# FFN entry of a one-core decoder layer: the first chunk's up tiles as a quad of seven block products

## The reference, cut to what matters

```python
hn = rms_norm(x, g_pre_ffn[l])
gu = jnp.einsum('bsd,df->bsf', hn, w_gate_up[l])
hf = jax.nn.silu(gu[..., :D_FF]) * gu[..., D_FF:]
ff = jnp.einsum('bsf,fd->bsd', hf, w_down[l])
x = x + rms_norm(ff, g_post_ffn[l])
```

## Time and profile before

| | us |
|---|---|
| median of 3 runs (1764.28 to 1937.19) | 1764.4 |
| the profiled execution | 1763.94 |
| its span | 1762.4 |
| TensorE busy | 1752.1 (99%) |
| VectorE busy | 1132.3 (64%) |
| ScalarE busy | 733.2 (42%) |
| GpSimd busy | 249.7 (14%) |

### The profile page before, as it was taken

The page is one execution under the profiler, slowest core; times in us unless marked ns, Lnnn a source line. Parts: engine busy times, 40 slices in busy tenths (PEclk is TensorE's granted clock), DMA queues, the critical chain, the costliest instruction groups (busy, mean ns, idle before and its releaser), DMA issues.

```text
span 1762.4 us, 23988 instructions
## 1 busy us (share of the span) xinstructions
PE 1752.1 (99%) x8497; PEld 1453.7 (82%) x8497; DVE 1132.3 (64%) x1927; ACT 733.2 (42%) x1486; POOL 249.7 (14%) x555
## 2 busy tenths in 40 slices
PE   9999999999999999999999999999999999999998
PEld 7888888888888888888888888888888888888886
DVE  5328888888775774443555655776656655567676
ACT  5316666666643233343221123343333333344553
POOL 3321222222210001111100112101011000000011
PEclk9999999999999999999999999999999999999999
DMA  7421222222143223337635712223233322673443
GB/s 244 144 85 57 76 74 73 73 73 72 49 144 95 72 66 130 104 102 259 219 132 167 240 60 83 96 96 142 93 111 109 105 89 102 228 279 100 145 143 126
DMA packets 138047, 213.80 MB, mean 121 GB/s; under 512 B 7569, under 2 KB 94097, under 8 KB 136930
## 3 DMA queue, kind: packets, MB, share of 16 engines
q1 hardware_dynamic: 109200, 108.54, 19.6%
q0 software_dynamic: 28752, 104.04, 16.2%
q10 hardware_dynamic: 2, 0.00, 0.0%
HBM read 150.17 MB, written 62.39 MB: 121 GB/s over the span
## 4 chain that ended last, share of the span: by engine, by line
PE 98%; DVE 1%; ACT 1%; DMA 0%; issue 0%; POOL 0%; POOLq 0%; DVEq 0%; ACTq 0%
PE ps L2343 26%; PE ps L2678 22%; PE ps L2546 17%; PE ps L2734 12%; PE ps L2427 10%; PE ps L2351 3%; PE ps L2443 3%; PE ps L2465 2%; PE ps L2467 1%; DVE ring L1564 0%; DMA x_tile<-in_x_dram 0%; ACT e_t L1089 0%; ACT ring L968 0%; DVE e_t L1667 0%; DVE d_op L1564 0%
## 5 line engine op out<-in xcount | busy, mean ns | idle before, releaser
L2734 PE MATMUL ps<-d_op 128*128 128x512 f32 x924 | 210.3, 389 | 0.1
L2734 PEld LDWEIGHTS ps<-d_op 128*128 128x128 f32 x924 | 173.3, 188 | 36.8 <-DVE d_op L1564 0.5
L2678 PE MATMUL ps<-s_op,t_op_T 128*128 128x512 f32 x720 | 169.9, 389 | 0.0
L2427 PE MATMUL ps<-xn,ring 128*128 128x512 f32 x672 | 167.0, 398 | 0.0
L2678 PEld LDWEIGHTS ps<-s_op,t_op_T 128*128 128x128 f32 x720 | 135.1, 188 | 28.1
L2427 PEld LDWEIGHTS ps<-xn,ring 128*128 128x128 f32 x672 | 122.3, 188 | 24.2
L2546 PE MATMUL ps<-s_op,x_op_T 128*128 128x512 f32 x576 | 135.9, 389 | 0.0
L2546 PEld LDWEIGHTS ps<-s_op,x_op_T 128*128 128x128 f32 x576 | 108.1, 188 | 22.5
L2678 PE MATMUL ps<-hn,t_op_B 128*128 128x512 f32 x480 | 115.1, 389 | 0.0
L2678 PEld LDWEIGHTS ps<-hn,t_op_B 128*128 128x128 f32 x480 | 90.1, 188 | 18.7
L1676 DVE CUSTOM_DVE_ANT_0 ps<-ps,mask 128x256 f32<-128x256 f32 (+7 forms) x128 | 94.5, 780 | 12.2 <-PE ps L2443 11.1
(11 more groups left out here) (270 smaller groups left out, 3361.4 us busy)
## 6 DMA issues: line engine op xcount, KB each, us to landing
pair<-in_w_gate_up_dram SPq DMA_DIRECT2D x20, 1024.0 KB, 5.2
rf_pieces<-s_scratch SPq DMA_DIRECT2D x74, 256.0 KB, 2.6
x_pair<-in_w_in_dram SPq DMA_DIRECT2D x16, 1024.0 KB, 6.7
raw<-in_w_in_dram SPq DMA_DIRECT2D x26, 512.0 KB, 4.0
s_scratch<-gated_ff POOLq DMA_DIRECT2D x40, 256.0 KB, 2.5
gate_in<-gate_scratch POOLq DMA_DIRECT2D x18, 512.0 KB, 3.6
v_scratch<-v_out POOLq DMA_DIRECT2D x32, 256.0 KB, 2.6
vh<-v_scratch POOLq DMA_DIRECT2D x16, 512.0 KB, 5.1
```

The costliest lines, as they stand in the source:

```text
L2427: last = pe.matmul(ps[:, proj_bank(first, half), :], proj_weights(which, par, a)[:, P * k:P * (k + 1)], xn[:, b, k, HALF * half:HALF * (ha ...
L2678: last = pe.matmul(ps[:, bank, :], t_op[name][:, a, k, :], block(b, k), start=opens and (k, a, b) == (0, HH, HH), stop=(k, a, b) == (3, LL ...
L2734: last = pe.matmul(ps[:, DOWN_BANKS[product][i], :], d_op[:, g % 4, a, P * i:P * (i + 1)], d_op[:, g % 4, 2 + b, :], start=opens and (a, b ...
```

## The change

Chunk 0's gate stays in plain tiles (4 groups), and its up becomes a quad of kind 1, the first of now 21. So the first quad uses `pair[1]`, has no B22 ahead (it runs third in the quad behind it), and is followed by a quad of kind 0. The silu of the four gate groups is put straight where the quads expect it (`first_gate`), and chunk 0 takes the way of all other chunks to the down projection: `h0_dram`, the loads back, `first_sums` and their stores are gone. GpSimd makes two of the `whole` values, s1's and s4's, when all rows of hn are in place; VectorE makes the other two, and waits for GpSimd's on `hn_wholes`.

```diff
-    GROUPS = G_FFN + 8
+    GROUPS = G_FFN + 4
...
-        QUADS = 2 * (FC - 1)
+        QUADS = 2 * FC - 1
...
             load(tile_of(w_gate_up, 0))
-            load(tile_of(w_gate_up, FF))
+            load(tile_of(w_gate_up, P))
...
             load_pair(0, True, 2 * P)
-            load(tile_of(w_gate_up, P))
-            load(tile_of(w_gate_up, P + FF))
             sp.wait_ge(w_lo, n.at())
-            load_pair(1, True, 2 * P + FF)
+            load_pair(1, True, FF)
+            load_pair(1, False, 2 * P + FF)
...
# GpSimd
-            for b in range(2):
-                pool.wait_ge(x1_stored[b], 16 * TT // 2)
-            for f in range(2):
-                pool.wait_ge(first_ready, 2 * f + 2)
-                pool.dma_start(h0_dram[P * f:P * (f + 1), :], hf_raw[:, :]).then_inc(first_stored, 16)
...
+            pool.wait_ge(groups_done, G_FFN)
+            pool.wait_ge(tr_free[0], TT + HEADS * TT + TT)
+            pool.wait_ge(tr_free[1], TT + HEADS * (TT + TT // 2) + TT)
+            for kept, half in ((1, 1), (4, 0)):
+                pool.tensor_tensor(s_raw[kept][:, HH], hn[:, HH, 4:8, HALF * half:HALF * (half + 1)].bitcast(F32),
+                                   hn[:, LL, 4:8, HALF * half:HALF * (half + 1)].bitcast(F32), ALU.add)\
+                    .then_inc(hn_wholes, 1)
...
# VectorE
             whole(s_raw[3][:, HH], hn, 0, 1)
             s_sum(3, s_raw[2][:, LL], s_raw[3][:, HH], ALU.subtract)
-            whole(s_raw[1][:, HH], hn, 1, 1)
-            hidden(0, 1)
-            split_next()
+            dve.wait_ge(hn_wholes, 1)
             s_sum(1, s_raw[3][:, HH], s_raw[1][:, HH], ALU.add)
...
-            whole(s_raw[4][:, HH], hn, 1, 0)
...
+            ff_quad(1, first=True)
             s_lo_of(4, 4)
-            ff_quad(0, first=True)
+            ff_quad(0)
             ff_quad(1)
-            first_sums()
...
# TensorE
-            for _ in range(2):
-                job(hn)
...
+            assert g.slot(4) == 0
             pe.wait_ge(s_lo, 1)
-            ff_quad(0, first=True)
-            for j in range(4):
+            for j in range(2):
                 wait_evacuated(pe, g, j - 4)
-            ff_quad(1, first=None)
+            ff_quad(1, first=True)
+            for j in (2, 3):
+                wait_evacuated(pe, g, j - 4)
+            ff_quad(0, first=None)
+            ff_quad(1)
```

More of the change, by code:

```diff
@@ L921, in store_chunk @@
                 made_n.next(4)
[L923 to L927, removed]
+            store_chunk(0)
+            with turns(pool, FC - 1, {hidden: 4, made_n: 4}) as it:
+                store_chunk(it + 1)
             for name in ("S3", "S1"):
-                pool.wait_ge(s_stored[name], 16 * FC)
+                pool.wait_ge(s_stored[name], 16 * (FC + 1))
             pool.dma_start(g_post_ffn_b[:, :], g_post_ffn[0, :].partition_broadcast(P)).then_inc(g3_landed, 16)
@@ L1410, in ff_quad @@
                 t_hi_of("T1", kind, True)
-                if kind == 1:
+                if kind == 1 and not first:
                     silu_of(1, 1).then_inc(silu_ready, 1)
@@ L1483, in _ @@
                 wait_evacuated(act, g, half - 2)
-            silu_half(0)
-            g.next()
-            silu_half(1)
-            split_next()
-            g.next()
+            first_gate(0, 0)
+            first_gate(1, 0)
             act.wait_ge(s_summed, 2)
             s_hi_of(3)
-            s_hi_of(1)
-            split_next()
+            act.wait_ge(pair_landed[1], 16)
+            t_hi_of("T3", 1, True)
+            t_hi_of("B11", 1)
+            first_gate(0, 1)
             act.wait_ge(s_summed, 3)
             s_hi_of(2)
[L1495 to L1499, removed]
-            for half in range(2):
-                silu_half(half)
-                if half == 0:
-                    act.wait_ge(s_summed, 4)
-                    s_hi_of(4)
-            t_hi_of("B21", 0)
-            t_hi_of("T2", 0, True)
-            t_hi_of("T4", 0, True)
-            g.next(2)
-            ff_quad(0, first=True)
+            t_hi_of("B21", 1)
+            t_hi_of("T2", 1, True)
+            s_hi_of(1)
+            first_gate(1, 1)
+            t_hi_of("T4", 1, True)
+            for j in range(4):
+                wait_evacuated(act, g, j - 4)
+            act.sem_inc(silu_ready, 3)
+            act.sem_inc(last_gate_read, 1)
+            act.wait_ge(s_summed, 4)
+            ff_quad(1, first=True)
+            s_hi_of(4)
+            ff_quad(0)
             ff_quad(1)
@@ L2169, in op_lo_of @@
                 lo(d_op[:, g % 4, 3, :], wd_piece(t_name, c), d_op[:, g % 4, 2, :]).then_inc(op_lo, 1)
-            def first_sums():
-                a11, a21, a12, a22 = (grid[:, HH, j, 1] for j in range(4))
-                dve.wait_ge(first_again[0], 48)
-                did(dve.tensor_tensor(a22, a21, a22, ALU.add))
-                did(dve.tensor_tensor(a21, a11, a21, ALU.subtract))
-                did(dve.tensor_tensor(a11, a22, a11, ALU.subtract))
-                did(dve.tensor_tensor(a12, a12, a11, ALU.subtract))
             def s_lo_of(kept, n_hi):
@@ L2713, in ff_quad @@
                 pe.wait_ge(t_lo, quad.at() * 7 + T_AT["T1"])
+                if first:
+                    pe.wait_ge(s_lo, 3)
                 pe.wait_ge(copied, quad.at() * 3 + 3)
```

90 lines of the change are left out of this document (26 added, 64 removed).

## The result

The changed kernel takes 1777.14 us (median of four runs, 1776.72 to 1777.83) where the kernel before takes 1764.34. The ratio is 1.0072, with a 95% interval of 1.0056 to 1.0088: 12.8 us or 0.7% slower. One of the four executions of the kernel before took 1937.19 us, a slow one that the ratio leaves out. 1776.1 had been forecast, with a range of 1765.0 to 1778.5. The profiled execution took 1776.72 us with a span of 1775.1, against 1762.4 before.

The account below looks back on a forecast made before the run. TensorE, on the path for 98% of the span, was taken to bound the kernel; 1763.94 - 2.79 (matmuls) + 3.4 (VectorE's chain) + 8.8 (GpSimd's adds) + 2.0 (clock) + 0.8 (B22) = 1776.1 us, range 1765.0 to 1778.5.

Parts of the forecast that it names:

- The matmuls: On TensorE, 96 up matmuls removed (21.83 us) and seven products added (19.04 us): a gain of 2.79 us.
- VectorE's chain without GpSimd: VectorE's instructions from the last row's low halves to T3's low half: 14.60 us, making TensorE's first product 3.4 us late.
- An add of 4.4 us: Length of each 2048-column GpSimd add, middle of 3.5 and 5.2 us; ends 1.8 and 5.2.
- the first rival: Short add: the exclusion holds but a GpSimd add takes 1.8 us, 1770.9 us; chance 0.17, shared with one add only in the way.
- The exclusion both ways: GpSimd's adds and VectorE's two-SBUF-input instructions shut each other out, so both adds stand in VectorE's chain: 8.8 us, ends 0 and 10.4.
- The second rival: No exclusion for a long GpSimd instruction, VectorE never waits: 1765.5 us, up to 1767.5; chance 0.17.
- The gap: TensorE idle ahead of the first quad's T3 product, released by VectorE's low half of T3: some 12 us.
- The clock: After the stall of some 12 us TensorE's clock falls to 1.2 GHz: 2.0 us lost on the way back, ends 0 and 4.
- B22 late by 0.8: First B22 product waits for s4's low half, ready 8.95 us behind T4's product where TensorE arrives after 8.16: 0.8 us.
- What costs nothing: Second pair's load, dropped tile loads, ring copies and DMAs, ScalarE's chain and the added waits: no cost or gain beyond terms counted.
- The rule for the ring's copies: ScalarE's and VectorE's two dropped ring copies fall away beside TensorE and give nothing.
- The third rival: Not slower: TensorE never waits and the 2.79 us gain stays, 1761.1 us; chance 0.03.

Follow-up runs that it names:

- The last kernel: Changed kernel without GpSimd adds, VectorE's work spread ahead of the last row, ScalarE copying the first quad's banks out before its high halves: 1762.16 us, ratio 0.9989.
- the memsets: Changed kernel with three GpSimd memsets of 2048 columns, which read nothing, in place of its second add: 1772.22 us, ratio 1.0043.
- the busy matmuls: Changed kernel with 50 extra TensorE matmuls into an unused bank ahead of the first quad's wait: 1778.22 us, ratio 1.0074.
- The two kernels with spread work: Changed kernel without GpSimd adds, VectorE's work spread ahead of the last row: 1764.87 us; the same with ScalarE's bank copies before its high halves: 1762.16 us.

## Why the prediction was right, and where not

- **The matmuls, -2.79.** Right. The last kernel shows it alone, less 0.76 that its rows account for, and there the time before the change is reached is as in the kernel before (1128.65 against 1128.67).
- **VectorE's chain without GpSimd, 14.60 us.** Right: 16.93 where it holds one value of 2.33 more.
- **An add of 4.4 us, ends 1.8 and 5.2.** Right: 4.36 from one add less, 4.19 from one add more. The memset of the same size takes 1.85, so the short add of the first rival, which took its rate from a memset, is out. The spans of the two adds in the profile are 6.6 each, not near 4.4 as the prediction said they would show: each holds a wait for a VectorE instruction too. The Trainium skill's 4497 ns (GPSIMD Engine Reference, section "Performance versus the Vector engine") is 3 to 7% above what these rows give.
- **The exclusion both ways.** Shown. One sum of VectorE goes from 2.28 to 6.6 us for each add, also for an add that no one needs, and none does for the memsets or where VectorE makes the values. This was the step with the widest room (0 to 8.8), and the Trainium skill's rule (SBUF — State Buffer, section "Who interferes with whom") decides it as the runs do. The second rival (1765.5) falls.
- **The gap: 12.2 forecast (3.4 + 8.8), 12.09 measured.**
- **The clock, 2.0.** 2.23 in the changed kernel's profile, at a granted clock of 0.50: the mechanism is right. The size was in part luck. It was taken from the program's start, where matmuls do stand at twice the usual interval (the first 5 of the 36 take 2.33 us), but the granted clock of the same kernel reads 1.00 in every window from 2 to 20 us, so those rows do not show the lower level; and behind the same kind of stall the other kernels lose 1.5 to 2.5. I also added it to the wait for s4 as if the two were independent. They are not, as the busy matmuls showed: with the clock kept, B22 starts at the same time.
- **B22 late by 0.8.** 0.73 measured, for a reason that doesn't hold. The prediction ties s4's low half to the end of T4's product by way of a steady quad (8.95 us behind it; 1179.41 - 1170.57 = 8.84 measured). With the clock kept, T4's product ends at 1169.10 and s4's low half still at 1179.38, 10.3 behind. VectorE is simply full from 1131 on. The right sum goes by VectorE's instructions up to s4's low half, and the clock's loss hides behind that; that both ways give 1776 to 1777 here is luck.
- **What costs nothing.** In the changed kernel none of those things waits. The rule for the ring's copies would have been different had the up tiles stayed, which the same adds in the kernel before showed (5.2 us).
- **The third rival, not slower,** needs the chain to end by 1142.3. In the changed kernel's order it can't; with most of the values made before the last row's low halves it ends at 1142.80, and the time is 1762.16.

## What to carry to other kernels

A GpSimd add that reads SBUF was no spare capacity here beside a VectorE whose instructions have two SBUF inputs: its whole length was added to VectorE's queue, at nearly twice what VectorE would need for the same add (4.36 against 2.29). Before work is given to another engine, ask whether VectorE has waits some 10 to 25 us earlier in which it could do it itself (here 3.96 and 4.37 us, ahead of 1109.24 and 1121.10); here that way, with the orders to match, is 15 us ahead of GpSimd's (1762.16 against 1777.14). Where an engine is late, count its instructions through to the last operand that the waiting engine asks for, not only to the first: terms that lie ahead of the same late operand don't add up.

## What the runs showed of the hardware

- **The clock falls after short waits, but not after all of them.** A wait of 2.90 us (the kernel before with GpSimd's values) was followed by 1.66 us lost, one of 2.01 by 1.64, and one of 1.99 by none: in the kernel with VectorE's values B22 took 1178.36 - 1175.51 = 2.85 us. Behind the first two the clock was still up when the matmuls began again (0.77 from 1146 to 1148, 0.89 from 1179 to 1181) and fell while TensorE was at work. It is not the kernel alone that decides: of four executions of the kernel kept busy in its stall, three took 1778.2 to 1778.4 at a mean granted clock of 0.998 and one 1776.33 at 0.999, 1.9 less; of nine of the kernel before with GpSimd's values, eight took 1768.65 to 1769.90 and one 1767.14. What decides it is open.
- **The loss costs 1.5 to 2.5 us in the first product.** After gaps of 5.5 to 16 us it took 4.24, 4.65, 4.70, 4.95, 5.11 and 5.26 us in six kernels instead of 2.72. The longest gap has 4.65, so it is not the gap's length that orders them. Each is from one execution; how far it differs between executions of one kernel is not shown.
- **The start of the program moves by a microsecond.** The first 36 matmuls with w_v stand at twice the usual interval for a part of their time, though the granted clock reads 1.00 there, and what follows them starts between 19.16 and 20.15 us in kernels whose code is the same up to there. The last gate matmuls begin later by about as much, from 1128.55 to 1129.56. The two kernels with spread work differ by 3.3 us in span: 0.86 from this start and 2.42 between it and B22. Their medians over eleven runs differ by 2.7, so that most of the 0.86 belongs to the execution that was profiled and not to the kernel. A span of a single execution should not be read finer than that.
- **Reading PSUM frees a VectorE instruction from the exclusion, as far as one instruction shows.** One input in PSUM and one in SBUF: 0.68 us at the start of GpSimd's add, as without it. That the add had begun is worked out from its length of 4.36 and its end.
